# A hybrid attention, DeltaNet and expert trunk on one core: another order of steps at the start, in the scan, in the router and in the norms

## The chip, the cores and the metric

The kernel runs on one core of one Trainium2 chip. The metric is the device time of one execution in microseconds (us); the kernel before was run three times. All arithmetic is in float32.

## The reference, cut to what matters

Two groups of tokens go through the same two layers: 128 context tokens and 512 sample tokens, 640 in all, of width 1024.

```python
for l in range(DEPTH):                                   # 2 layers
    sh1, sc1, ga1, sh2, sc2, ga2 = adaln(cond, w_mod[l], b_mod[l])      # silu(cond) @ w_mod + b_mod
    p = rmsnorm(x, g_norm1[l]) * (1 + sc1) + sh1
    glu, q, k, v, dn_qkv, dn_z, dn_ab = split_projection(p @ w_in[l])
    out_a = conformer_conv(glu, ...)                     # depthwise convolution of 31 taps
    out_b = attention(q, k, v, ...)                      # neighbourhood (sample) or full (context)
    out_c = gated_deltanet(dn_qkv, dn_z, dn_ab, ...)     # chunked scan, forward and backward
    x = x + ga1 * (concat(out_a, out_b, out_c) @ w_out[l])
    h = rmsnorm(x, g_norm2[l]) * (1 + sc2) + sh2
    gates = top2_of_best_group(h @ router_wg[l], h @ router_we[l])      # 16 experts in 4 groups
    x = x + ga2 * sum_e gates[e] * (silu(h @ w1[l,e]) * (h @ w3[l,e])) @ w2[l,e]
y = rmsnorm(x, g_final)
```

The outputs are y for both groups, the context's keys and values, and the final states of the scan.

## The kernel before, in words

The kernel is written as one program per engine (`@block.sync`, `tensor`, `scalar`, `vector`, `gpsimd`); each runs its instructions in the order of the text, and semaphores (`need(signal, n)`, `wait_ge`) tie them together. That written order and the semaphores are what sets the order of the work; there is no planner. Two layers are unrolled in Python.

- **Tiles.** x is kept transposed, `xT` (128 partitions x 8 tiles of features x 640 tokens). `hT` (in `hreg`) holds squares, then the normalized x. Weights go through three ring buffers of 2 MB, filled by SP's queue.
- **Start.** SP loads all constants, x, c and c_ctx, then the four first modulation loads (`ring_load(("mod", n))`, 2 MB each), then the input projection's weights. TensorE (PE) turns x. ACT's queue issues the 17 small loads of parameters (`load_params`, L1203) and the copy of the relative bias (L1232) when c has been turned. PE multiplies the four modulation loads (`mod_rows`, L618; `mod_turn`, L624), then turns the parameters (L638, L639), then sums the squares of x over features with a matmul of ones (`norm_sums`, L645, L646). DVE clears three padded buffers (L1597, L1598) at the layer's start, adds the modulation's bias (L1614, L1616) and multiplies x by the inverse root (`norm_one`, L1620); ACT scales and shifts (L1251, L1252); the projection is L656 and L657.
- **DeltaNet.** Five chunks j of 128 tokens, two directions d. Between chunks, PE turns the block inverse (`turn_inverse`, L852) that POOL computes in 30 small steps (`diag_inverse`, L2202, L2203) and DVE spreads into blocks (`inverse_spread`, L1827). Before it, DVE updates the state of both directions (L1913, L1918 or L1921); behind it follow the level matmuls (L865, L876, L878). POOL also prepares decayed keys and queries (L2181, L2174).
- **Router.** After the output projection (L1022, L1023) the squares are summed, the logits of 20 columns made in two matmuls per token chunk (L1049 and, for a constant row, L1050), and DVE selects groups and experts in many small steps (L1991 to L2021). Normalization 2 is shared: DVE has tiles 0 and 1 (tile 1 after the selection), POOL tiles 2 to 7 (L2232). PE sums ranks (L1055 to L1058) and turns the tokens (L1069); they are stored to `hx`, gathered for the first blocks (L2239) and scattered to `xs` (L2249). `turn_block` (L1081) turns a block of gathered tokens, ACT copies it (L1501).
- **Experts.** A loop over at most 13 pairs of blocks with `If`/`Else` on the number in use; 8 or 9 are in use. ACT stores each block's output to `ys` (L1505). In the `Else` branch every engine only advances its semaphores; ACT waits there for the stores (L1534).
- **Combination.** POOL gathers each token's two outputs (L2259) when all stores and empty slots have been counted; DVE weighs them per chunk of 128 tokens (`weigh`, L2108, L2109), PE turns the sum (L1158), DVE adds it to `xT` (L2121). After the fifth chunk comes the next layer's normalization, or the final one: squares over all 640 tokens (L1543), sums (L1164, L1165), root (L1545, L1547), product (L2126), transposes to token layout (L1172), copies (L1551), and two stores of y (L1554, L1555).

The lines that a sentence can't give are the end of `norm(1)` on ACT and the empty slots:

```python
for k in range(KD) if n == 0 else (0, 2, 3, 4, 1, 5, 6, 7):      # order of the scaled tiles
    if n == 0:
        need(norm_x, k + 1)              # DVE's product
    elif k < 2:
        need(norm_x, KD + k + 1)
    else:
        need(norm_xp, k - 1)             # POOL's product
...
with act.Else():
    for sig, n in ((sil_ready, 0), (xg_copied, 2), (hid_copied, 0)):
        wait(pr, sig, n, 2)
        act.sem_inc(sig.sem, 2)
    for q in range(2):
        wait(pr, ys_stored[q], 0, 16)
        act.sem_inc(ys_stored[q].sem, 16)
```

## Time and profile before

| what | value |
|---|---|
| median of 3 runs | 2068.96 us (2057.93 to 2071.48) |
| profiled execution, its own time | 2063.77 us |
| span in the profile, first to last instruction | 2061.7 us, 22012 instructions |
| granted TensorE clock, mean | 0.905 |
| PE busy | 1758.6 us (85%) |
| DVE, ACT, POOL busy | 845.3, 476.1, 286.3 us |

The profile is of one execution. PE is the TensorE's matmuls, PEld its weight loads, DVE, ACT and POOL the vector, scalar and GpSimd engines, SP the engine that issues most loads; a trailing q stands for an engine's issue of DMAs. Times in rows are us from the start of the span.

### The profile page before, as it was taken

What the parts mean: (1) busy time and instruction counts of PE and PEld (TensorE: products, weight loads), DVE (VectorE), ACT (ScalarE), POOL (GpSimd) and SP (SyncE); (2) the same over time, 40 slices, a digit from 0 to 9 for tenths busy, and PEclk for the clock granted to TensorE, in tenths of its full rate; (3) what the DMA queues carried; (4) which work ended last, traced back from release to release, by engine and by line L of the source; (5) the groups of instructions that cost most, each with busy time, mean ns of one, the idle gap of its engine ahead of it and who ended that gap; (6) DMA issues with size and microseconds to landing.
All of it is one profiled execution on the core that took longest, in us unless ns stands there. A gap on an engine that the chain in (4) does not pass through costs nothing. (4 is left out here: it accounts for less than half of the span.)

```text
span 2061.7 us, 22012 instructions
## 1 busy us (share of the span) xinstructions
PE 1758.6 (85%) x8309; PEld 1129.0 (55%) x8309; DVE 845.3 (41%) x1626; ACT 476.1 (23%) x850; POOL 286.3 (14%) x450
## 2 busy tenths in 40 slices
PE   4899996987988985999589999797889888699965
PEld 2455663645877553554345566464678844454433
DVE  2169304556666322111326930456576533211114
ACT  1211003353221212222031110335322021222112
POOL 0000213013442012000220000001442201200010
PEclk8899997998999996999689999898899998799986
DMA  9321796920000107999552111450000010799952
GB/s 356 61 82 41 238 281 226 345 72 1 1 1 1 53 21 260 373 362 379 185 132 82 41 62 41 136 211 1 1 1 1 1 53 21 293 386 365 370 210 106
DMA packets 113911, 301.80 MB, mean 146 GB/s; under 512 B 27904, under 2 KB 35746, under 8 KB 100642
## 3 DMA queue, kind: packets, MB, share of 16 engines
q1 hardware_dynamic: 65424, 218.16, 28.5%
q0 software_dynamic: 14080, 53.48, 7.8%
q10 hardware_dynamic: 34322, 28.99, 4.9%
q8 instruction: 58, 0.95, 0.2%
q14 instruction: 27, 0.22, 0.0%
HBM read 234.51 MB, written 67.05 MB: 146 GB/s over the span
## 5 line engine op out<-in xcount | busy, mean ns | idle before, releaser
L656 PE MATMUL ps<-hreg,ring 128*128 128x512 f32 x768 | 399.5, 602 | 7.7 <-ACT hreg L1252 7.7
L657 PEld LDWEIGHTS ps<-hreg,ring 128*128 128x128 f32 x768 | 147.7, 192 | 187.1 <-issue 187.1
L1097 PE MATMUL ps<-ring,tok 128*128 128x512 f32 x544 | 238.3, 596 | 0.5 <-issue 0.4
L1097 PEld LDWEIGHTS ps<-ring,tok 128*128 128x128 f32 x544 | 103.9, 192 | 131.5 <-issue 131.5
L657 PE MATMUL ps<-hreg,ring 128*128 128x128 f32 x768 | 149.0, 276 | 0.0
L656 PEld LDWEIGHTS ps<-hreg,ring 128*128 128x128 f32 x768 | 118.6, 195 | 8.0 <-issue 8.0
L1112 PE MATMUL ps<-ring,work 128*128 128x512 f32 x272 | 122.4, 592 | 0.0
L2087 DVE TENSOR_TENSOR work<-work,ps 128x256 f32<-128x256 f32 x34 | 14.3, 421 | 252.8 <-ACT work L1510 252.8
L1649 DVE SCALAR_TENSOR_TENSOR mixA<-cin_reg,small,mixA 128x655 f32<-128x655 f32 x120 | 107.1, 895 | 0.0
L2091 DVE COPY zs<-ps 128x1024 f32<-128x1024 f32 x34 | 41.6, 1225 | 119.9 <-PE ps L1112 119.9
L2164 POOL TENSOR_TENSOR hreg<-dnT,cst 128x512 f32<-128x512 f32 x16 | 20.4, 1274 | 483.8 <-DVE dnT L1851 483.8
L1663 DVE SCALAR_TENSOR_TENSOR tmp_reg<-mixb_reg,small,tmp_reg 128x642 f32<-128x642 f32 x96 | 84.7, 882 | 0.0
L1112 PEld LDWEIGHTS ps<-ring,work 128*128 128x128 f32 x272 | 49.1, 191 | 48.8 <-issue 48.8
L1081 PE MATMUL ps<-cst,tok 128*128 128x128 f32 x304 | 43.8, 291 | 29.7 <-DMA tok<-hx,idx 27.5
L2259 POOL DMA_INDIRECT hreg<-ys,slots x10 | 11.8, 1180 | 406.3 <-ACTq L1535 403.8
L1022 PE MATMUL ps<-dnT,ring 128*128 128x512 f32 x128 | 65.5, 594 | 0.0
L1158 PE MATMUL ps<-cst,hreg 128*128 128x128 f32 x80 | 19.6, 427 | 49.2 <-DVE hreg L2109 49.2
L852 PE MATMUL ps<-cst,ring 128*128 128x128 f32 x80 | 17.6, 368 | 47.6 <-DVE ring L1827 47.6
L1081 PEld LDWEIGHTS ps<-cst,tok 128*128 128x128 f32 x304 | 39.7, 197 | 30.7 <-issue 27.6
L1287 ACT ACTIVATE mixb_reg<-ps 128x512 f32<-128x512 f32 x24 | 14.3, 597 | 174.1 <-PE ps L657 174.1
L1945 DVE SCALAR_TENSOR_TENSOR xT<-ps,small,xT 128x512 f32<-128x512 f32 x16 | 12.0, 751 | 103.4 <-PE ps L1023 103.4
L618 PE MATMUL ps<-ring,small 128*32 128x512 f32 x384 | 48.7, 629 | 6.6 <-DMA ring<-in_w_mod 4.9
(350 smaller groups left out, 3058.0 us busy)
## 6 DMA issues: line engine op xcount, KB each, us to landing
ring<-in_w SPq DMA_DIRECT2D x102, 1024.0 KB, 8.1
ring<-in_w_mod SPq DMA_DIRECT2D x24, 2048.0 KB, 8.3
ring<-in_w_in SPq DMA_DIRECT2D x12, 2048.0 KB, 7.9
ys<-zs ACTq DMA_DIRECT2D x34, 512.0 KB, 7.9
tok<-xs SPq DMA_DIRECT2D x30, 512.0 KB, 9.5
xs<-zero POOLq DMA_DIRECT2D x8, 1792.0 KB, 19.6
ys<-zero POOLq DMA_DIRECT2D x8, 1664.0 KB, 18.5
ring<-in_w_out SPq DMA_DIRECT2D x4, 2048.0 KB, 8.0
```

Of the source, the lines that this page charges most:

```text
L618: ins = mm(bank(bnk)[32 * j:32 * j + 32], condT[:, k, :], w[:, k, :], start=k < 4, stop=k >= 4)
L656: mm(o[:, 0:TS], lhs(k), rhs(k)[:, 0:TS], start=k == 0, stop=k == nk - 1)
L657: ins = mm(o[:, TS:T], lhs(k), rhs(k)[:, TS:T], start=k == 0, stop=k == nk - 1)
L1022: mm(gslot(gg % 2)[:, 0:TS], lhs, mix(k)[0], start=k == 0, stop=k == KD - 1)
L1081: ins = turn(ps[:, P * k:P * (k + 1)], xg[q].rearrange("p (m k) -> p k m", k=KD)[:, k], ident)
L1097: ins = mm(bank(2 + q), xgT[q][:, k, :], w, start=k == 0, stop=k == KD - 1)
L1112: ins = mm(bank(4 + 2 * q + n), hidT[:, P * f:P * (f + 1)], ring[2][:, 2048 * q + D * f + 512 * n:2048 * q + D * f + 512 * n + 512], start ...
L1158: ins = turn(ps[:, o:o + P], yg[0][c_][:, P * k:P * (k + 1)], ident)
L1649: last[t] = count(V.scalar_tensor_tensor(mixA[:, t, :], src, w, mixA[:, t, :], ALU.mult, ALU.add))
L1663: ins = V.scalar_tensor_tensor(out, src, w, out, ALU.mult, ALU.add)
L2091: V.tensor_copy(ysb[q], ps[:, 2048 + 1024 * q:3072 + 1024 * q]).then_inc(y_out.sem, 1)
L2164: G.tensor_tensor(rcos[t % 2], dnT[:, qk_tile(t), 0:TS], cst[:, C_COS:C_COS + TS], ALU.mult).then_inc(rope_cos.sem, 1)
```

## The change

1. **Start.** The constants are loaded in three pieces, the cosine, sine and mask tables behind the third modulation load. c and c_ctx are loaded into `dsm`. ACT issues the parameter loads and the bias copy of layer 0 before its first wait. In layer 0 the square sums are made between the modulation matmuls into the first banks, and the parameters are turned behind the third modulation; DVE's memsets follow the modulation's sums.
2. **Scan.** `inverse_spread(j + 1)` stands between the two directions' state updates.
3. **Router.** The constant row is spread over partitions by two matmuls inside the output projection and added by DVE when it reads the logits. DVE makes tiles 0 to 3 of normalization 2 before the selection, POOL tiles 4 to 7. The second `turn_block` uses other banks.
4. **Empty slots.** ACT counts the stores without waiting for them there.
5. **Norms after the experts.** Squares and sums of layer 1's first normalization are made per chunk. The final one is made in token layout: per chunk a transpose, a square with its row sum, logarithm and exponential of one column, one product with the gain from a loaded row, one store by SP.

```diff
+            for a, b in ((0, C_COS), (C_COL, NC)):
+                sp.dma_start(cst[:, a:b], consts[:, a:b]).then_inc(once["cst_loaded"], 16)
...
-            sp.dma_start(prm[0:8, 0, :], c[0].rearrange("(k p) -> k p", p=P)).then_inc(once["first_loaded"], 16)
+            sp.dma_start(dsm[0:8, 0:P], c[0].rearrange("(k p) -> k p", p=P)).then_inc(once["first_loaded"], 16)
...
                     for n in range(MOD_FIRST):
                         ring_load(("mod", n))
+                        if n == 2:
+                            sp.dma_start(cst[:, C_COS:C_COL], consts[:, C_COS:C_COL]).then_inc(once["cst_loaded"], 16)
...
+                if l == L - 1:
+                    sp.dma_start(g_row, g_final.rearrange("(a n) -> a n", a=1).to_broadcast([P, D])).then_inc(once["g_loaded"], 16)
...
+            for c_ in range(NCH):
+                sp.wait_ge(once["fin_y"], c_ + 1)
+                rows_ = y_sample[0][tokens(c_), :] if c_ < TS // P else y_prompt[0]
+                sp.dma_start(rows_, yg[0][c_]).then_inc(once["y_stored"], 16)
...
                         if n:
                             mod_turn(n - 1, first_rows[n - 1], 3072 + 8 * (n - 1))
+                        if n == 1:
+                            norm_sums(range(0, 4), 0)
+                        if n == 2:
+                            norm_sums(range(4, KD), 0)
+                            params_turn()
                     mod_turn(3, first_rows[3], 3072 + 24)
...
+                    if m == 2:
+                        need(logit_copied, 1)
+                        for g_ in range(2):
+                            ins = mm(ps[:, 2940 + 20 * g_:2960 + 20 * g_], ident[0:2, g_:g_ + 1].to_broadcast([2, P]), crow,
+                                     start=True, stop=True)
...
-                    mm(o, lrow[:, P * t:P * (t + 1)], route_c[:, X_SEL:X_SEL + 20], start=True, stop=False)
-                    ins = mm(o, ident[0:2, g_:g_ + 1].to_broadcast([2, P]), crow, start=False, stop=True)
+                    ins = mm(o, lrow[:, P * t:P * (t + 1)], route_c[:, X_SEL:X_SEL + 20], start=True, stop=True)
...
-                need(xg_copied, 1)
                 need(xf_loaded[1], 16)
-                turn_block(1)
+                turn_block(1, 2048)
...
+                def next_sums(c_):
+                    pe.wait_ge(sq_ready.sem, sq_ready.at(l + 1, c_ + 1 if c_ + 1 < NCH else KD))
+                    for k in range(KD):
+                        ins = mm(ps[:, 2048 + P * c_:2048 + P * (c_ + 1)], ones, yg[0][c_][:, P * k:P * (k + 1)],
+                                 start=k == 0, stop=k == KD - 1)
...
+                def last_turn(c_):
+                    need(comb_added, c_ + 1)
+                    if c_ >= 2:
+                        pe.wait_ge(once["fin_y"], c_ - 1)
+                    for k in range(KD):
+                        o = 2048 + 1024 * (c_ % 2) + P * k
+                        ins = turn(ps[:, o:o + P], xT[:, k, tokens(c_)], ident)
+                    ins.then_inc(once["y_turned"], 1)
+                finish = next_sums if l + 1 < L else last_turn
...
+                    if c_:
+                        finish(c_ - 1)
+                finish(NCH - 1)
...
+            load_params(0)
+            bias_copy(0)
+            act.wait_ge(once["cst_loaded"], 32)
...
-                    for k in range(KD) if n == 0 else (0, 2, 3, 4, 1, 5, 6, 7):
+                    for k in range(KD):
...
+                        for q in range(2):
+                            act.sem_inc(ys_stored[q].sem, 16)
                         for sig, n in ((sil_ready, 0), (xg_copied, 2), (hid_copied, 0)):
...
-                        for q in range(2):
-                            wait(pr, ys_stored[q], 0, 16)
-                            act.sem_inc(ys_stored[q].sem, 16)
+                nc.scalar.preload_act_table_set("natural_log_exp_and_others")
+                if l + 1 < L:
+                    for c_ in range(NCH):
+                        need(comb_added, c_ + 1)
+                        A_(yg[0][c_].rearrange("p (k n) -> p k n", k=KD), xT[:, :, tokens(c_)], ACT.Square)\
+                            .then_inc(sq_ready.sem, 1 if c_ + 1 < NCH else KD + 1 - NCH)
...
+            for c_ in range(NCH):
+                act.wait_ge(once["y_turned"], c_ + 1)
+                A_(yg[0][c_], ps[:, 2048 + 1024 * (c_ % 2):3072 + 1024 * (c_ % 2)], ACT.Square,
+                   accum_out=fin_ss[:, c_:c_ + 1]).then_inc(once["fin_sq"], 1)
+                act.wait_ge(once["fin_sq"], 2 * c_ + 1)
+                A_(fin_rs[:, c_:c_ + 1], fin_ss[:, c_:c_ + 1], ACT.Ln, scale=1.0 / D, bias=eps_c).then_inc(once["fin_sq"], 1)
+                act.wait_ge(once["fin_sq"], 2 * c_ + 2)
+                A_(fin_rs[:, c_:c_ + 1], fin_rs[:, c_:c_ + 1], ACT.Exp, scale=-0.5).then_inc(once["fin_r"], 1)
...
-                for s in stage:
-                    V.memset(s, 0.0)
-                V.memset(cin_reg[:, :], 0.0).then_inc(pads_zeroed.sem, 1)
...
                 V.scalar_tensor_tensor(A[0], mod[:, 8:16, :], 1.0, both[:, R_G1:R_G1 + KD].to_broadcast([P, KD, 2]),
                                        ALU.add, ALU.mult).then_inc(mod_ready.sem, 1)
+                if l == 0:
+                    dve.wait_ge(once["cst_loaded"], 48)
+                for s in stage:
+                    V.memset(s, 0.0)
+                V.memset(cin_reg[:, :], 0.0).then_inc(pads_zeroed.sem, 1)
...
                     for d in range(2):
+                        if d == 1 and j < 4:
+                            inverse_spread(j + 1)
...
-                    if j < 4:
-                        inverse_spread(j + 1)
...
+                    if m == 3:
+                        need(logit_rows, 2)
+                        V.tensor_copy(crb[:, 0:4, :], ps[:, 2940:2960].rearrange("p (a n) -> p a n", a=1).to_broadcast([P, 4, 20]))
+                        step(V.tensor_copy(crb[:, 4, :], ps[:, 2960:2980]))
...
-                norm_one(0)
+                for k in range(4):
+                    norm_one(k)
...
-                norm_one(1)
...
+                def last_norm(c_):
+                    dve.wait_ge(once["g_loaded"], 16)
+                    dve.wait_ge(once["fin_r"], c_ + 1)
+                    V.scalar_tensor_tensor(yg[0][c_], ps[:, 2048 + 1024 * (c_ % 2):3072 + 1024 * (c_ % 2)], fin_rs[:, c_:c_ + 1],
+                                           g_row, ALU.mult, ALU.mult).then_inc(once["fin_y"], 1)
...
+                    if l == L - 1 and c_:
+                        last_norm(c_ - 1)
+                if l == L - 1:
+                    last_norm(NCH - 1)
...
-                for k in range(2, KD):
+                for k in range(4, KD):
                     G.tensor_tensor(hT[:, k, :], xT[:, k, :], rst, ALU.mult).then_inc(norm_xp.sem, 1)
```

## Rows read from the trace of the kernel before

**Rows 1.** PE's waits: line, releaser, us in total, times, longest.

```profile
PE ps L852 <- DVE ring L1827: 47.6, 18, 7.3
```

**Rows 2.** Timeline of the start: start, us, engine, line, operation, count, idle before.

```profile
22.68 1.28 DVE L1597 MEMSET mixb_reg<- 128x646 f32 x2 [0.20 <-DVE xT L1569]
...
23.36 0.40 ACTq L1203 DMA_DIRECT2D tmp_reg<-in_b_mod  x1
...
37.34 3.19 PE L618 MATMUL ps<-ring,small 128*32 128x512 f32 x16 [2.87 <-DMA ring<-in_w_mod]
...
40.46 1.95 PE L624 MATMUL ps<-cst,work 128*128 128x2 f32 x16
...
54.66 0.47 PE L638 MATMUL ps<-cst,tmp_reg 128*128 128x128 f32 x1 [12.26 <-DMA small<-in_router_we]
...
68.79 5.97 DVE L1620 TENSOR_TENSOR hreg<-xT,rst 128x640 f32<-128x640 f32 x8 [12.69 <-ACT rst L1242]
...
71.00 2.04 PE L656 MATMUL ps<-hreg,ring 128*128 128x512 f32 x2 [3.83 <-ACT hreg L1252]
```

**Rows 3.** Stretches: busy by engine, PE clock, DMA share, GB/s.

```profile
5.00:10.00 5.00, 0.00 (x0) 0.00 (x0) 0.00 (x0) 0.00 (x0) 0.00 (x0) 1.00 0.98 399
...
35.00:40.00 5.00, 2.66 (x16) 0.68 (x16) 0.00 (x0) 0.00 (x0) 0.00 (x0) 0.66 1.09 351
```

**Rows 4.** Timeline of the first chunk boundary of the DeltaNet, layer 0.

```profile
529.38 0.68 DVE L1918 COPY dnT<-ps 128x512 f32<-128x512 f32 x1
...
530.10 1.04 POOL L2181 TENSOR_TENSOR tmp_reg<-tok,small 128x512 f32<-128x512 f32 x1
...
532.65 2.93 DVE L1827 TENSOR_TENSOR ring<-dsm,cst 128x512 f32<-128x512 f32 x2
534.06 0.63 PE L852 MATMUL ps<-cst,ring 128*128 128x128 f32 x4 [3.08 <-DVE ring L1827]
...
536.61 1.91 PE L865 MATMUL ps<-work,hreg 128*128 128x128 f32 x8
```

**Rows 5.** Stretches around two chunk boundaries and one behind the scan.

```profile
526.00:546.00 20.00, 15.87 (x116) 15.50 (x115) 12.95 (x32) 6.00 (x14) 8.09 (x17) 0.83 0.00 1
565.00:585.00 20.00, 15.88 (x127) 15.51 (x126) 13.77 (x34) 6.00 (x14) 8.57 (x19) 0.91 0.00 1
686.00:688.00 2.00, 0.29 (x1) 0.29 (x2) 0.94 (x2) 1.62 (x3) 0.00 (x0) 1.00 0.33 115
```

**Rows 6.** Timeline of the routing, layer 0.

```profile
764.86 9.58 POOL L2232 TENSOR_TENSOR hreg<-xT,rst 128x640 f32<-128x640 f32 x6 [116.64 <-ACT rst L1242]
765.56 1.52 DVE L1620 TENSOR_TENSOR hreg<-xT,rst 128x640 f32<-128x640 f32 x1
...
771.53 1.45 DVE L1993 SCALAR_TENSOR_TENSOR small<-small,cst 128x20 f32<-128x20 f32 x1
...
783.68 6.87 PE L1069 MATMUL ps<-cst,hreg 128*128 128x128 f32 x40 [2.49 <-ACT hreg L1252]
...
810.45 1.97 PE L1081 MATMUL ps<-cst,tok 128*128 128x128 f32 x8 [1.11 <-ACT tok L1501]
```

**Rows 7.** DMA issues behind layer 0's last pair: queue, count, KB each, us to landing.

```profile
ys<-zs ACTq DMA_DIRECT2D x2, 512.0 KB, 2.6
```

**Rows 8.** Timeline from layer 0's last store to layer 1's projection.

```profile
998.25 0.34 ACTq L1505 DMA_DIRECT2D ys<-zs  x1
1005.65 0.95 POOL L2259 DMA_INDIRECT hreg<-ys,slots  x1 [191.44 <-ACTq L1535]
...
1029.66 4.31 DVE L2121 SCALAR_TENSOR_TENSOR xT<-ps,small,xT 128x128 f32<-128x128 f32 x16
...
1053.17 1.53 PE L656 MATMUL ps<-hreg,ring 128*128 128x512 f32 x2 [3.84 <-ACT hreg L1252]
```

**Rows 9.** Timeline of the last layer's combination.

```profile
2014.98 1.28 DVE L2109 SCALAR_TENSOR_TENSOR hreg<-dnT,small,hreg 128x1024 f32<-128x1024 f32 x1
...
2024.28 4.30 DVE L2121 SCALAR_TENSOR_TENSOR xT<-ps,small,xT 128x128 f32<-128x128 f32 x16
```

More of the change, by code:

```diff
@@ L599, in _ @@
                 ins.then_inc(once["pe_first"], 1)
-            turn(bank(4, 16), prm[0:16, 0, :], ident[0:16, 0:16]).then_inc(once["cond_turned"], 1)
+            turn(bank(4, 16), dsm[0:16, 0:P], ident[0:16, 0:16]).then_inc(once["cond_turned"], 1)
             pe.wait_ge(once["x_turned"], KD)
@@ L626, in mod_turn, with params_turn, norm_sums @@
                     ins.then_inc(mod_turned, 1)
+                def params_turn():
+                    need(prm_loaded, 16 * PRM_DMAS)
+                    turn(bank(7, P), prm[:, 0, :], ident)
+                    turn(ps[:, 3584 + P:3584 + P + NROW2], prm[0:NROW2, 1, :], ident[0:NROW2, 0:NROW2]).then_inc(prm_turned.sem, 1)
+                def norm_sums(tiles, lo):
+                    for k in tiles:
+                        need(sq_ready, k + 1)
+                        mm(ps[:, lo:lo + TS], ones, hT[:, k, 0:TS], start=k == 0, stop=k == KD - 1)
+                        ins = mm(ps[:, lo + TS:lo + T], ones, hT[:, k, TS:T], start=k == 0, stop=k == KD - 1)
+                        if k == KD - 1:
+                            ins.then_inc(norm_ss.sem, 1)
                 if l == 0:
@@ L1542, in _ @@
-            for k in range(KD):
-                A_(hT[:, k, :], xT[:, k, :], ACT.Square).then_inc(once["fin_sq"], 1)
-            act.wait_ge(once["fin_ss"], 1)
-            A_(rst[:, 0:T], ps[:, 2048:2048 + T], ACT.Ln, scale=1.0 / D, bias=eps_c).then_inc(once["fin_r"], 1)
-            act.wait_ge(once["fin_r"], 1)
-            A_(rst[:, 0:T], rst[:, 0:T], ACT.Exp, scale=-0.5).then_inc(once["fin_r"], 1)
-            yt = xload
-            for k in range(KD):
-                act.wait_ge(once["y_turned"], k + 1)
-                A_(yt[:, :, k * P:(k + 1) * P], gslot(k % 2).rearrange("p (c n) -> p c n", c=NCH), ACT.Copy)\
-                    .then_inc(once["y_copied"], 1)
```

102 lines of the change are left out of this document (39 added, 63 removed).

## The prediction, made before the changed kernel was run

> **What bounds the kernel now.** I read the waits of TensorE (PE) first, then the timeline at the places they name, then windows there for the granted clock. PE is busy most of the time, so what can be won lies where it stands still. Five kinds of place do that, and the change touches each: the start, the chunk boundaries of the DeltaNet scan, the routing, the passage from layer 0 to layer 1, and the end. The reader should see in each group which instruction ends the wait.
>
> *Start* [rows 2]: the last of four modulation loads (mod 3) is used at 37.34, its rows are turned by 42.4, but PE then stands 12.26 us until 54.66 for the parameter list, whose first load was issued only at 23.36. Then come the two parameter transposes, the modulation sums on DVE, the square sums, the root, the product with it (68.79) and the first projection matmul at 71.00. The transfers behind this fill the DMA engines [rows 3].
>
> *DeltaNet* [rows 1, 4]: at a chunk boundary PE waits for inverse_spread (L1827), 47.6 us in 18 waits; two per layer belong to the first chunk and are not touched, leaving four boundaries per layer.
>
> *Routing, passage, end* [rows 6 to 9]: PE waits for normalized tiles, for the stores of the experts' outputs, for a whole normalization after the last combined chunk.
>
> **Start.** The parameter list is issued ahead of everything on ACT's queue, c and c_ctx get a place of their own (dsm), and 1 MB of constants goes behind mod 2. The bytes ahead of mod 3 stay the same, but the whole list now shares the engines with them. Before, part of it did so after mod 3. DMA moved 399 GB/s without the list and 351 GB/s with it [rows 3]: 12% of the 31.3 us from its first issue to its landing is 3.8 us; I charge mod 3 with 1 us (bounds 0 and 4). So mod 3 at 38.3; its rows 3.2 (41.5); copy and turn 1.9, as from 40.53 to 42.41 (43.4); two small DVE operations, taken as 0.4 (estimate; they lie in the 1.5 us from 54.66 to the square sums that the code puts behind them). The squares and square sums need no parameter and move between the modulation matmuls, where PE waited for loads. The three memsets of the padding, before under a DVE that stood idle, now stand behind the modulation sums and ahead of the product: two at 0.64 and one of 1370 columns, by columns 1.36, so 2.6 us in all (46.4). From the product's start to the first matmul is 2.2 (68.79 to 71.00): 48.6. Gain 22.4. What is queued behind the memsets on DVE is exactly that product, so they are paid in full. ACT can start its first function only when it has issued 18 DMAs; from the first issue to the last landing is 31.3, which bounds that issue from above, and I take 21 (estimate), about when x has been turned. Bounds of the start: 13 (issue or DMA cost 10 more) to 24.
>
> A rule of the skill speaks against this part. The Trainium skill, "DMA: Bandwidth & Descriptors", section "Specifications", asks for transfers of 512 B or more for line rate; router and gate rows are 16 to 64 B. By it the list could cost the engines more than the 12%; the trace agrees that there is a loss, and rival C carries what it would do.
>
> **DeltaNet boundaries.** inverse_spread(j+1) moves ahead of the state update of direction 1. DVE is through with direction 0 at 530.06 and POOL's inverse is done at about 530.1 [rows 4], so it can run at once instead of at 532.65. POOL's next operation (530.10, 1.04 us) holds it up: the two spreads took 2.93 beside POOL, each ending about 0.6 behind the end of one POOL operation. So direction 0 ends at 531.8 (before 534.06) and direction 1 at 532.8. Two transposes and a copy later L865 starts at 533.7 against 536.61: 2.9 us each. The state update of direction 1 slips by 2.6 us; its reader comes after some ten matmul groups, so that costs nothing; if POOL were late, it would be the first to be late too. At the fourth, ahead of the context's chunk, two memsets of the state stand there as well and no row is shown; between 0 and 2.9 I take 1.7. Per layer 3x2.9+1.7 = 10.4, both 20.8.
>
> Then the clock. PE idles 3 us there and its granted clock falls: over 20 us it was 0.83 or 0.91; of the first three boundaries of both layers two read like the one row, four like the other [rows 5]. At the lower level (1.2 of 2.4 GHz) that is 6.8 us and 3.6 us, of which half is lost: 2x3.4+4x1.8 = 14. After the change PE idles about 0.8 and 0.5. The nearest row is 686 to 688: busy only 0.29 of 2 us, clock 1.00 throughout [rows 5]. I take it that the clock stays: 14 back (bounds 0 and 20).
>
> The Trainium skill, "TensorE: Matmul & The Clock Gate", section "A second HAM failure mode: psum-queue depth-cycling", tells of short idle spells between matmul groups that come often enough to make the clock swing between its levels. By that rule nothing of the 14 would come back; the row of 686 speaks against it here. It is rival B.
>
> **Routing.** POOL's share of the products falls from six tiles to four (6.4 us instead of 9.58), DVE takes four at once instead of one and, after the selection, another [rows 6]. Beside POOL such a product took 1.52 where the eight at the start took 0.75, and a DVE operation of 20 columns 1.45 while POOL ran: two-input operations end up waiting for POOL's. So DVE is through at 765.56+4x1.52 = 771.6, POOL at 771.3, and the selection's small steps, which before were held until 774.4, run free: about 1.2 us sooner. ACT has all eight tiles by about 778 (five scalings behind 771.6, each at most the 1.4 that the 2.2 at the start leave beside a product), ahead of the ranks. PE's token transposes no longer wait 2.49 for it (783.68). The second block's transposes go to other banks, so the wait of 1.11 at 810.45 goes. 2.5+1.2+1.1 = 4.8, less two small matmuls (0.6, estimate) that the router's constant row adds inside the output projection: 4.2 per layer, 8.4 in both (bounds 4 and 13). The row's removal from the logits saves only what the four products already cover: nothing. DVE's two table copies lie under a projection group: nothing.
>
> **Passage.** In the empty expert slots ACT waited for the last store and then ran through its slots: store issued 998.25 with 0.34, landing 2.6 later (1001.2), gather called 0.8 ahead of 1005.65. The slots' 3.65 us now start at 998.6 and overlap the landing: 2.6 sooner, in both layers [rows 7, 8].
> The last addition ends at 1033.97 (T), the first matmul comes at 1053.17: 19.2. After: one square of 1024 columns 1.1; eight 128-column matmuls, 3.8 at the lower clock by the nearest row (four took 1.91 [rows 4]) or 1.9 at full; the parameter transposes and DVE's pieces 1.5; memsets 2.6; product to matmul 2.2: T+11.2 or T+9.3. Gain 8.0 to 9.9; I take 9. The other four chunks' squares and sums lie under DVE's weighing; the second table load and the bias copy under PE's sums. 11.6 in all.
>
> **End.** Adds end at 2028.58 now [rows 9]. After: 2.6 sooner by the stores; three products with the final gain ahead of the last add, each 1.28 plus 0.03 by the 128x1024 operation: 2029.9. Then eight transposes 2.0 (as at 810.45), square 1.1, two one-column functions 0.5, the last product 1.3, store issue and landing 0.34+2.6, which was the price of the same 512 KB in [rows 7]; some 0.6 to the end: 2038.4 against 2061.7. Gain 23.3 (bounds 20 and 25). The four other stores and the load of the final gain lie under this or under the projection.
>
> **Sum.** 22.4+20.8+14+8.4+11.6+23.3 = 100.5 off the profiled execution's 2063.8: 1963. The runs shown have their median 5 above that execution and their fastest 6 below, so I name 1965, and the range goes by it. DVE, ACT and POOL work that the change moves is hidden elsewhere by PE's matmuls; the dense stages and expert pairs, most of the time, are unchanged.
>
> **Rivals.**
> A, the forecast: 1950 to 1982, 0.60.
> B, the clock still falls at the boundaries: 14 less, 1979; 0.18.
> C, the list's small rows hold the modulation loads up: 10 more, mod 3 at 48, 1975; 0.09. For: engines are full there. Against: the list landed within 31 us beside 8 MB of loads.
> D, the change does not do what it says in the DeltaNet: the spread waits for POOL as long as before, or the delayed update is missed. PE then waits as now: 35 less, 2000; 0.08. For: POOL's end and DVE's are within 0.1 us. Against: POOL's next operations are of 1.04 us, and one of them is all it waits for.
> E, slower: PE, fed earlier, is granted the lower clock in the dense projections. Each such microsecond loses half; it decides from 2x100 us on, slower by over 1% from about 240. At 300 us: 1963+150 = 2113. Against: at every boundary it was back at full within 6.8 us [rows 5]. 0.02.
> The remaining 0.03: several gains at their lower bounds, inside or near 1%.
>
> Range 1943 to 1992: A with its bounds and the runs' spread, B, C. Beyond it lie D, E and the rest, and A's ends. A measurement of this kernel can tell about 1% from no change; faster by over 1%: 0.95, within 1%: 0.03, slower: 0.02.
>
> **What would show it.** First projection matmul near 49 (C: near 58, with the third modulation's matmuls late); L852's wait near 1 us and windows of 20 us behind it with the clock near 1.00 (B: still 0.83 to 0.91; D: waits of 3 us); transposes in the routing directly behind the rank sums; about 10 us between the last addition of layer 0 and the projection; 10 us from the last addition to the end instead of 33. Wrong would be: a new wait of PE for the update of direction 1, DVE's product behind memsets later than 47, or the adds of the last layer slower than 5.5 us a chunk.

## The result, and the profile after

The changed kernel took 1987.8 us (median of 4 runs, 1983.3 to 1990.7) against 2066.3 for the kernel before (4 runs on the same chip, 2057.9 to 2071.5): a ratio of 0.962, 95% interval 0.958 to 0.966. The span fell from 2061.7 to 1984.7 us. The prediction was 1965, range 1943 to 1992, faster at 0.95. The direction is as forecast and the time is in the range, but the gain is 77 us where the sum had 100.5. Where the other 23 went is what the experiments are for.

The first lines of the page after the change, and PE's longest waits (line, releaser, us in total, times, longest):

```profile
span 1984.7 us, 22021 instructions
...
PE 1726.3 (87%) x8313; PEld 1109.2 (56%) x8313; DVE 856.5 (43%) x1631; ACT 473.9 (24%) x850; POOL 287.3 (14%) x446
```

```profile
PE ps L1203 <- DVE hreg L2148: 36.5, 6, 15.4
PE ps L875 <- DVE ring L1863: 32.0, 20, 7.4
PE ps L1108 <- DMA tok<-hx,idx: 27.1, 4, 12.7
PE ps L1082 <- DVE small L2062: 21.0, 2, 10.5
...
PE ps L1130 <- DVE work L2126: 2.2, 1, 2.2
```

L875 is the L852 of [rows 1]: 47.6 us of waiting became 32.0, of which 15.9 are the waits at the first chunk (7.4 and 0.6 in each layer), which nothing touched. L1082 and L1130 are new or longer: PE waits 10.5 us a layer for the selection (8.1 at most before), and once for the first block's product.

**Stages.** The next table is worked out from the timelines: the first start of one line to the first start of another on PE, in us, both layers where there are two numbers. Lines of the changed kernel: first projection matmul L680; projection and attention L680 to L849; scan L849 to L1023; selection L1070 to L1096; first pair L1124 to L1139; passage L1203 to L680; end from L1203 in layer 1 to the end of the span. The kernels e1 to e9 are the experiments below.

| kernel | first matmul | proj. + attention | scan | selection | first pair | passage | end |
|---|---|---|---|---|---|---|---|
| before | 71.0 | 390.8 / 378.5 | 218.7 / 221.1 | 21.8 / 22.3 | 15.9 / 15.8 | 38.8 | 52.3 |
| e7, before + move | 70.4 | 392.5 / 379.1 | 205.8 / 205.8 | 22.3 / 22.3 | 17.7 / 15.7 | 38.3 | 52.3 |
| after | 52.6 | 394.5 / 381.7 | 206.2 / 206.2 | 19.3 / 19.3 | 18.3 / 15.6 | 29.6 | 30.9 |
| e1, move undone | 53.9 | 390.8 / 381.7 | 218.7 / 216.8 | 19.3 / 19.3 | 19.7 / 15.1 | 29.1 | 30.7 |
| e2, POOL holds | 55.5 | 394.0 / 382.7 | 197.5 / 198.9 | 19.2 / 19.3 | 17.9 / 15.5 | 28.8 | 31.1 |
| e3, memsets early | 51.5 | 394.1 / 379.7 | 207.7 / 205.0 | 19.3 / 19.3 | 19.3 / 16.3 | 26.3 | 31.5 |
| e4, small rows late | 50.0 | 394.5 / 381.8 | 208.7 / 203.5 | 19.3 / 19.3 | 18.7 / 14.9 | 29.3 | 30.2 |
| e5, DVE alone | 54.5 | 394.6 / 382.7 | 207.0 / 206.0 | 17.5 / 17.5 | 19.7 / 15.1 | 29.7 | 30.8 |
| e6, list early | 53.1 | 393.9 / 381.5 | 207.9 / 206.2 | 19.3 / 19.3 | 16.6 / 16.0 | 29.3 | 31.7 |
| e8, four together | 46.2 | 394.0 / 381.6 | 201.8 / 199.1 | 17.5 / 17.5 | 18.0 / 15.0 | 27.1 | 30.8 |
| e9, and list cut | 46.8 | 393.9 / 378.1 | 199.4 / 198.9 | 17.5 / 17.5 | 16.0 / 16.1 | 26.4 | 31.2 |

The columns that an edit doesn't touch show how far one execution differs from another: 1 to 2 us in most, about 4 to 5 in projection and attention.

### The profile page after: what moved, and what is told of

The parts are those of the page before. It is cut to its first block and busy times, and to the rows that moved or that the text cites. A ratio compares the mean times of both kernels' runs of the same rounds, so it can differ in the third digit from the quotient of the medians.

```text
span 1984.7 us, 22021 instructions
## 1 busy us (share of the span) xinstructions
PE 1726.3 (87%) x8313; PEld 1109.2 (56%) x8313; DVE 856.5 (43%) x1631; ACT 473.9 (24%) x850; POOL 287.3 (14%) x446
## 5 line engine op out<-in xcount | busy, mean ns | idle before, releaser
L680 PE MATMUL ps<-hreg,ring 128*128 128x512 f32 x768 | 401.7, 605 | 11.1 <-ACT hreg L1291 11.1
L1124 PE MATMUL ps<-ring,tok 128*128 128x512 f32 x544 | 237.9, 595 | 0.2 <-issue 0.2
L1124 PEld LDWEIGHTS ps<-ring,tok 128*128 128x128 f32 x544 | 103.9, 191 | 130.9 <-issue 130.9
L680 PEld LDWEIGHTS ps<-hreg,ring 128*128 128x128 f32 x768 | 119.0, 196 | 11.4 <-issue 11.4
L1139 PE MATMUL ps<-ring,work 128*128 128x512 f32 x272 | 122.4, 592 | 0.0
L1139 PEld LDWEIGHTS ps<-ring,work 128*128 128x128 f32 x272 | 49.1, 191 | 48.8 <-issue 48.8
L1108 PE MATMUL ps<-cst,tok 128*128 128x128 f32 x304 | 43.8, 291 | 27.1 <-DMA tok<-hx,idx 27.1
L1540 ACT ACTIVATE tok<-ps 128x1024 f32<-128x1024 f32 x38 | 38.9, 1025 | 51.7 <-PE ps L1108 48.0
L633 PE MATMUL ps<-ring,small 128*32 128x512 f32 x384 | 47.3, 614 | 3.8 <-issue 2.1
## 6 DMA issues: line engine op xcount, KB each, us to landing
xs<-zero POOLq DMA_DIRECT2D x8, 1792.0 KB, 19.7
```

Of the source, the lines that this page charges most:

```text
L633: ins = mm(bank(bnk)[32 * j:32 * j + 32], condT[:, k, :], w[:, k, :], start=k < 4, stop=k >= 4)
L680: mm(o[:, 0:TS], lhs(k), rhs(k)[:, 0:TS], start=k == 0, stop=k == nk - 1)
L1108: ins = turn(ps[:, a + P * k:a + P * (k + 1)], xg[q].rearrange("p (m k) -> p k m", k=KD)[:, k], ident)
L1124: ins = mm(bank(2 + q), xgT[q][:, k, :], w, start=k == 0, stop=k == KD - 1)
L1139: ins = mm(bank(4 + 2 * q + n), hidT[:, P * f:P * (f + 1)], ring[2][:, 2048 * q + D * f + 512 * n:2048 * q + D * f + 512 * n + 512], start ...
L1540: A_(xgT[q], ps[:, a:a + D].rearrange("p (k n) -> p k n", k=KD), ACT.Copy).then_inc(xg_copied.sem, 1)
```

## The experiments

Each is the changed kernel with the edit shown, except e7. Ratios are to the kernel before on the same chip; for the changed kernel it was 0.9622.

### e1: the move in the scan undone; e7: the move alone

```diff
-                        if d == 1 and j < 4:
-                            inverse_spread(j + 1)
...
+                    if j < 4:
+                        inverse_spread(j + 1)
```

> The changed kernel with one part undone: inverse_spread(j + 1) stands again behind both directions' state updates, as in the kernel before. In the two traces the stretch from the first chunk's level matmuls to the end of the scan is 11.5 us shorter after the change in layer 0 and 14.9 us in layer 1, of which about 2.5 us in layer 1 fall before the first boundary and belong to the clock there. Theory: the move alone makes the rest, 22 to 25 us, most of it as waits of TensorE (2.8 us at each of six boundaries, 0.7 to 1.3 at the two ahead of the context's chunk), the clock's part being about 5. Then this kernel takes about 2011 us (2009 to 2014), with waits of about 3.1 and 1.0 us at each boundary and low-clock stretches of 3.4 to 6.8 us at all of them. Rival, the forecast's own term: 35 us, 2023. Second rival, the scan became shorter because of something else that moved it (the clock's phase, say): under 10 us, below 1998.

e7 is the same edit the other way round, in the kernel before.

> The kernel before with one part of the change alone: inverse_spread(j + 1) between the two directions' state updates. Theory: the move makes the scan 12 to 13 us shorter in each layer (218.7 and 221.1 us from its first matmul to the output's norm in the kernel before, 206.2 in both layers after) and no other stage differs by more than its granted clock: 25 us less than before, 2036 (2033 to 2039). Rival, the forecast's term: 35 less, 2026. Second rival, a part of the scan's gain in the changed kernel hung on the other parts: 15 or less, 2046 and more. Its other stages are a second look at the kernel before: the stretch from the first projection matmul to the scan was 390.8 and 378.5 us there and 390.8 to 394.5 and 379.7 to 382.7 in five profiles with the change. If it is within 1 us of 390.8 and 378.5 again, the change has lengthened that stretch by some 3 us a layer; if it is nearer to 394 and 382, the difference is that of single executions.

e1 took 2008.2 us, ratio 0.9738 [0.9706, 0.9770]; e7 took 2040.2, ratio 0.9885 [0.9861, 0.9909]. Taken away from the one it costs 0.0116 and given to the other it gains 0.0115: 24 us both ways, so the move works by itself and does not hang on the other parts. The 35 of the forecast is out. (e1's time lies just under the 2009 to 2014 expected of it; the 24 us by the ratios lie within the 22 to 25.) PE's waits for the spread, in e1 and then in e7:

```profile
PE ps L875 <- DVE ring L1863: 47.2, 18, 7.3
...
PE ps L852 <- DVE ring L1827: 31.6, 20, 7.3
```

Some 15 to 16 of the 24 us are these waits (47.2 to 32.0, and 47.6 to 31.6); about 8 remain for the clock. Stretches of 20 us from the first two boundaries of layer 0 (PE, PEld, DVE, ACT, POOL busy, PE clock, DMA share, GB/s), after the change and then in e1:

```profile
510.00:530.00 20.00, 17.64 (x140) 16.89 (x139) 16.13 (x39) 6.00 (x14) 8.86 (x18) 0.91 0.00 1
549.00:569.00 20.00, 17.65 (x145) 15.71 (x144) 18.12 (x36) 4.96 (x13) 6.51 (x9) 1.00 0.01 1
...
510.00:530.00 20.00, 15.88 (x116) 15.51 (x114) 12.54 (x30) 5.81 (x14) 7.31 (x14) 0.83 0.00 1
549.00:569.00 20.00, 15.53 (x122) 14.96 (x120) 13.77 (x33) 5.99 (x14) 7.79 (x16) 0.91 0.00 1
```

e1 has the clock of [rows 5] again, 0.83 and 0.91. After the change it was 0.91 at the first and 1.00 at the second boundary (and at the third, in both layers). Over both scans PE is busy 363.4 us in e1 and 355.6 after the change, with the same number of matmuls: these 7.8 us are the clock's part.

### e2: POOL holds until both spreads are made

```diff
                     diag_inverse(j + 1)
+                    need(dn_xt, 2 * (j + 1) + 2)
                     key_decay(j + 1)
```

> The changed kernel with one wait added: POOL begins the decayed keys of the next chunk only when DVE has made both spreads. In the trace of the changed kernel the two spreads take 2.96 us beside POOL's key operations, and TensorE waits 0.90 and 0.82 us for them at a boundary; the shortest such spread in the kernel before, without a POOL operation beside it, took 0.69. Theory: the spreads are slow only because POOL runs beside them. Alone they take 0.7 each, direction 0 is ready 0.8 us sooner and direction 1 1.6 us sooner, TensorE's two waits nearly go: 1.5 us at each of six boundaries and perhaps 0.5 to 1.5 at the two ahead of the context's chunk, 10 to 12 us in all: about 1977 us. Rival: POOL's keys and queries, begun 1.4 us later, become what TensorE waits for within the chunk, and the gain is given back: 1985 to 1992, with a new wait for POOL. Second rival: the spreads take 1.5 us without POOL as well (their shape, not POOL, sets it): no change in their mean, 1988 to 1995.

1973.5 us, ratio 0.9567 [0.9536, 0.9597]: 11 us less than the changed kernel, with intervals that just overlap. First boundary of layer 0, the timeline after the change and then in e2:

```profile
514.48 1.04 POOL L2226 TENSOR_TENSOR tmp_reg<-tok,small 128x512 f32<-128x512 f32 x1
514.56 2.96 DVE L1863 TENSOR_TENSOR ring<-dsm,cst 128x512 f32<-128x512 f32 x2 [0.17 <-POOL dsm L2248]
515.48 1.49 POOL L2226 TENSOR_TENSOR rst<-tok,small 128x512 f32<-128x512 f32 x1
516.22 0.63 PE L875 MATMUL ps<-cst,ring 128*128 128x128 f32 x4 [0.90 <-DVE ring L1863]
517.67 0.63 PE L875 MATMUL ps<-cst,ring 128*128 128x128 f32 x4 [0.82 <-DVE ring L1863]
518.13 1.08 PE L888 MATMUL ps<-work,hreg 128*128 128x128 f32 x6
...
516.80 1.29 DVE L1863 TENSOR_TENSOR ring<-dsm,cst 128x512 f32<-128x512 f32 x2
517.63 1.23 PE L875 MATMUL ps<-cst,ring 128*128 128x128 f32 x8
518.17 1.04 POOL L2226 TENSOR_TENSOR tmp_reg<-tok,small 128x512 f32<-128x512 f32 x1 [1.41 <-DVE ring L1863]
519.04 1.13 PE L888 MATMUL ps<-work,hreg 128*128 128x128 f32 x8 [0.18 <-ACT work L1454]
```

Two spreads take 2.96 us beside POOL and 1.29 alone; PE's two waits are gone (L875 runs its eight transposes in one go). POOL begins 1.4 later and its operations are 1.04 each instead of 1.04 and 1.49, and no wait for POOL appears. The waits for L1863 fall from 32.0 to 19.2 us, by 12.8, and the scan from 206 to 198 in each layer, by 16 in these two profiles. The rest of the 16 goes with the clock, which stayed at full over all boundaries of both layers (1.00 from 510 to 640 and from 1450 to 1580). By the ratios of the runs the gain is 11 us, inside the 10 to 12 expected.

The Trainium skill, "SBUF — State Buffer", section "Who interferes with whom", says that a DVE operation with two SBUF inputs contends with a GpSimd operation that reads SBUF, and that what they share is an exclusive lock. This pair agrees, 2.96 us against 1.29.

### e3: memsets at the layer's start

```diff
                 need(gemm_done, 0)
+                for s in stage:
+                    V.memset(s, 0.0)
+                V.memset(cin_reg[:, :], 0.0).then_inc(pads_zeroed.sem, 1)
```

> The changed kernel with the three memsets of the padding back at the start of the layer, ahead of the modulation copies, where DVE stands idle. Theory: in the changed kernel they stand between the modulation sums and the product and are paid in full: 47.85 to 50.48 in layer 0, and in layer 1 the product starts at 12.26 after the hundred (1012.26) where the root is there at 1010.06. Gone from there, the first projection matmul comes 2.6 us sooner in layer 0 and 2.2 in layer 1: 4.8 in all, about 1983 us. Rival: something else ends just behind (the weights of the projection, the root), and less than 1.5 us in all is won: 1987.

1981.2 us, ratio 0.9602 [0.9572, 0.9633]; the intervals overlap, so the stages decide. The passage is 26.3 instead of 28.8 to 29.7 in the others with the memsets where the change put them: 3. In layer 0 the fourth modulation came at 45.10 there, 1.6 later than after the change, and the first matmul 1.1 sooner: 2.7. The two lines in e3 (those after the change stand under e4):

```profile
45.10 1.93 PE L633 MATMUL ps<-ring,small 128*32 128x512 f32 x16
...
51.53 1.99 PE L680 MATMUL ps<-hreg,ring 128*128 128x512 f32 x2 [2.63 <-ACT hreg L1291]
```

Both as the theory says: the memsets were paid in full.

### e4: small rows and the bias copy behind the first weights

```diff
-            load_params(0)
-            bias_copy(0)
+            load_params(0, act, True, False)
...
                     ring_load(("in", l, c_))
+                    if l == 0 and c_ == 0:
+                        bias_copy(0, sp)
+                        load_params(0, sp, False, True)
```

The first call issues the ten loads that PE turns, the second the other seven, which have a semaphore of their own.

> The changed kernel with only the ten parameter loads that TensorE turns issued at the start; the other seven loads of the list (rows of 16 to 64 bytes, about 3,700 packets) and the copy of the bias go to SP's queue behind the first weights of the input projection. The third modulation is used at 34.53 and the fourth at 43.46 in the changed kernel, against 30.08 and 37.34 before, and the transfers moved 328 to 362 GB/s from 5 to 30 us against 367 to 402 before. Theory: the small rows hold up the modulation loads. Without them the fourth is used 2.5 to 4 us sooner (39.5 to 41), the first projection matmul comes at 49 to 50 instead of 52.6, and the time is about 1984.5. Rival: the loss comes from the ten loads of 512-byte rows and from the constants being cut into pieces of shorter rows; then the rate from 5 to 15 us stays at about 330 and the fourth modulation at 42.5 or later: 1987 or more. Second rival: the first weights or the bias, held up by the small rows, come too late, and the start is no sooner or later than 52.6.

1982.7 us, ratio 0.9610 [0.9579, 0.9642]; again the stages decide. The rate of the transfers, after the change and then in e4:

```profile
10.00:15.00 5.00, 0.09 (x1) 0.12 (x2) 0.00 (x0) 0.00 (x0) 0.00 (x0) 1.00 0.96 328
20.00:25.00 5.00, 2.86 (x20) 2.00 (x18) 3.50 (x5) 1.38 (x2) 0.00 (x0) 1.00 1.11 350
...
10.00:15.00 5.00, 0.49 (x3) 0.52 (x4) 0.00 (x0) 0.00 (x0) 0.00 (x0) 1.00 1.04 392
20.00:25.00 5.00, 3.08 (x26) 2.06 (x28) 3.11 (x4) 2.17 (x3) 0.00 (x0) 1.00 1.05 387
```

So the small rows do slow the transfers. But in most profiles that is not what the start waits for. Timeline after the change (L633 multiplies the modulation loads), then the fourth modulation and the first matmul in e4, then the first modulation in e1:

```profile
17.49 6.01 ACTq L1215 DMA_DIRECT2D bias_pad<-in_na_rel_bias  x1
23.61 1.28 ACT L1248 ACT_TABLE_LOAD   x1 [23.61 <-PE ps L615]
25.19 3.64 PE L633 MATMUL ps<-ring,small 128*32 128x512 f32 x32 [2.09 <-issue]
34.53 1.92 PE L633 MATMUL ps<-ring,small 128*32 128x512 f32 x16 [0.28 <-DMA ring<-in_w_mod]
43.46 1.92 PE L633 MATMUL ps<-ring,small 128*32 128x512 f32 x16 [1.42 <-DMA ring<-in_w_mod]
50.48 5.90 DVE L1656 TENSOR_TENSOR hreg<-xT,rst 128x640 f32<-128x640 f32 x8
52.62 2.05 PE L680 MATMUL ps<-hreg,ring 128*128 128x512 f32 x2 [5.36 <-ACT hreg L1291]
...
40.81 1.92 PE L668 MATMUL ps<-ring,small 128*32 128x512 f32 x16
49.97 2.05 PE L715 MATMUL ps<-hreg,ring 128*128 128x512 f32 x2 [5.36 <-ACT hreg L1298]
...
27.02 4.98 PE L633 MATMUL ps<-ring,small 128*32 128x512 f32 x32 [4.07 <-issue]
```

PE waits 1.70 us for modulation loads after the change, and not at all in e1, e2, e3, e5, e6 and e4. In the first five of those it waits 3.6 to 5.2 us ("issue") in front of the first modulation, because ACT's SiLU stands behind ACT's own DMA issues, which end there at 24.4 to 25.6; the first modulation then runs in part at the lower clock (4.98 us in e1, 3.64 after the change). Behind that PE is busy without a gap: eight pairs of square sums of 1.08 each, 8.7 us, lie between the modulations. e4 takes the issues away and the small rows at once, so that no run parts the two. By the timelines it was the issue in those five: their fourth modulation comes at 43.96 to 46.37, 3 to 6 us later than in e4, without a wait for a load. After the change itself it was the loads, 1.70 of the 2.65 us; there ACT's issues ended at 23.50, only 0.4 us behind PE's last transpose ahead of the SiLU (L615).

### e5: all eight products of normalization 2 on DVE

```diff
-                for k in range(4):
+                for k in range(KD):
                     norm_one(k)
...
-                for k in range(4, KD):
-                    G.tensor_tensor(hT[:, k, :], xT[:, k, :], rst, ALU.mult).then_inc(norm_xp.sem, 1)
```

> The changed kernel with all eight products of normalization 2 on DVE ahead of the selection, none on POOL. In the changed kernel four products on DVE and four on POOL run side by side and both engines take 1.94 us for each (7.76 and 7.77 us), and DVE reads the logits only at 748.54; at the start of the layer DVE alone took 5.90 us for eight, 0.74 each. Theory: the two engines hinder each other, and DVE alone is through with eight sooner than both with four: at 740.86 + 5.9 = 746.8. The small steps, the ranks and the token transposes come 1.8 us sooner in both layers, ACT's eight scalings (1.09 each) end at about 751, ahead of the ranks: 3.6 us, less what layer 0 gives back where ACT issues the next layer's loads: 1984 to 1986. Rival: DVE takes 1.5 or more for each product beside ACT's scalings too, and the selection starts at 753 or later: 1996 or more. Second rival: the scalings end after the ranks and hold up the token transposes: no gain, 1988.

1983.7 us, ratio 0.9601 [0.9576, 0.9626]. Timeline of layer 0, after the change and then in e5:

```profile
740.16 7.77 POOL L2277 TENSOR_TENSOR hreg<-xT,rst 128x640 f32<-128x640 f32 x4 [118.18 <-ACT rst L1281]
740.86 7.76 DVE L1656 TENSOR_TENSOR hreg<-xT,rst 128x640 f32<-128x640 f32 x4
748.54 0.25 DVE L2039 TENSOR_TENSOR small<-ps,work 128x100 f32<-128x100 f32 x1
753.82 0.71 PE L1082 MATMUL ps<-small,cst 128*128 128x80 f32 x2 [10.51 <-DVE small L2062]
...
743.01 5.96 DVE L1653 TENSOR_TENSOR hreg<-xT,rst 128x640 f32<-128x640 f32 x8
748.89 0.26 DVE L2036 TENSOR_TENSOR small<-ps,work 128x100 f32<-128x100 f32 x1
754.18 0.71 PE L1081 MATMUL ps<-small,cst 128*128 128x80 f32 x2 [9.74 <-DVE small L2059]
```

One engine makes eight products in 5.96 us; two engines make four each in 7.77. The selection takes 17.5 us instead of 19.3 in both layers, the 1.8 expected. In the time it is 4 us, with overlapping intervals.

### e6: the next layer's list ahead of the token copies

```diff
+                if l + 1 < L:
+                    load_params(l + 1)
                 copy_tokens(0, 0)
                 copy_tokens(0, 1, 2048)
-                if l + 1 < L:
-                    load_params(l + 1)
```

> The changed kernel with the loads of layer 1's parameters issued before ACT's two copies of gathered tokens instead of behind them. In layer 0 of the changed kernel ACT issues these 17 loads from 782.77 to 796.64 (11.4 us in the kernel before, 13.9 here), its first SiLU comes only at 799.14, and TensorE waits 2.18 us for the product behind it; the stretch from the first up projection to the first down projection is 18.3 us in layer 0 and 15.6 in layer 1, where no list is issued. Theory: the list stands ahead of the SiLU on ACT's queue and took back 2.5 us of what the routing had gained. In the 15.6 us that ACT waits for the gathered tokens it costs nothing: that stretch falls to 15 to 16 us in layer 0, the time to about 1985. Rival: the list's small rows then share the engines with the scattered and gathered tokens, TensorE waits longer than 12.5 us for the first block, and nothing is won: 1988 or more. Second rival: the first up projection, not ACT, sets that stretch: no change.

1991.0 us, ratio 0.9650 [0.9625, 0.9676]: nothing won, rather some 6 us lost by the ratio (the intervals overlap). ACT's queue and what waits for it, after the change and then in e6:

```profile
793.61 1.89 ACTq L1241 DMA_DIRECT2D small<-in_w_in  x1
795.52 1.12 ACTq L1241 DMA_DIRECT2D small<-in_router_we  x1
797.85 1.28 ACT L1549 ACT_TABLE_LOAD   x1 [14.06 <-issue]
800.04 0.50 PE L1130 MATMUL ps<-cst,work 128*128 128x128 f32 x2 [2.18 <-DVE work L2126]
...
773.66 9.41 ACTq L1241 DMA_DIRECT2D small<-in_w_in  x1
783.10 9.52 ACTq L1241 DMA_DIRECT2D small<-in_router_we  x1
793.74 15.61 PE L1124 MATMUL ps<-ring,tok 128*128 128x512 f32 x32 [7.79 <-ACT tok L1540]
```

The theory was right that the list sets the first pair (18.3 fell to 16.6) and wrong on the idle 15.6 us: beside the scatter of tokens, two loads took 9.4 and 9.5 us to issue instead of 1.9 and 1.1, and PE stood 7.8 us for ACT's copies.

### e8 and e9: what the experiments point to

e8 has the edits of e2 to e5 together. In e9 ACT issues, besides, only ten of layer 1's loads, and SP the other seven behind layer 1's first weights.

> The changed kernel with four of the edits together: POOL waits for both spreads, the memsets stand at the layer's start, the small rows and the bias copy go to SP's queue behind the first projection weights, and DVE makes all eight products of normalization 2. Alone they gave, as differences of the ratio to the kernel before, 0.0055, 0.0020, 0.0012 and 0.0021, together 0.0108 of 2062, 22 us. Theory: the places don't touch each other (scan, start and passage, start, routing), so the gains add: a ratio of about 0.951 (0.949 to 0.954), 1964 us. In the profile: first projection matmul at 47 to 48, scan 198 us in both layers, 17.5 us from the square sums to the token transposes. Rival: with the start's loads sooner and the memsets gone, the first projection weights or ACT's scalings set the start (first matmul still at 50), and layer 0's routing gain goes to the wait behind ACT's list of loads (18 to 20 us from the first up projection to the first down projection, as in all runs with the list there): 1968 to 1972.

The edit of e9, against e8:

```diff
-                    load_params(l + 1, act, True, True)
+                    load_params(l + 1, act, True, False)
...
-                        load_params(0, sp, False, True)
+                        load_params(l, sp, False, True)
```

> The four edits together, and in layer 0 ACT issues only the ten turned parameter loads of layer 1 behind the copies of gathered tokens; the seven others follow on SP's queue behind the first projection weights of layer 1. From the first up projection to the first down projection layer 0 took 17.7 to 19.7 us in all profiles with 17 loads in ACT's queue there and 14.9 to 16.3 in layer 1 without. The seven loads are 5 to 6 of ACT's 13.9 us of issue. Theory: ACT's issue sets that stretch, so with ten loads it ends before the first up projection is through (half of it is there 12.3 us after its start) and the stretch falls to 15 to 16 us: 3 us less than the four edits alone, about 1961. Rival: ten loads are still too long or something else delays the SiLU: the stretch stays at 18 or more and the time equals that of the four edits. Second rival: the seven loads, now in front of layer 1's later projection weights, delay these or the gathered outputs, and it is slower than the four edits.

e8: 1960.2 us, ratio 0.9489 [0.9466, 0.9513]. e9: 1955.9, ratio 0.9465 [0.9441, 0.9490]. The gains add, 27 us by the ratio where the four alone had given 22: first matmul at 46 to 47, scan near 199 to 202, selection 17.5. In e9 the first pair of layer 0 takes 16.0 instead of 18.0, as expected, though the two intervals overlap. Both are faster than the changed kernel and than the one before it.

## Why the prediction was right, and where it was off

The time lies in the stated range, but above case A's 1950 to 1982, to which the prediction gave 0.60. The upper end of the range took in rivals B and C, and neither came out in the main. That the time is still inside, at 1988, owes something to luck. What held is the direction and most of the mechanisms; four terms came out smaller than forecast. One of the signs that the prediction named for being wrong did appear: DVE's product behind the memsets came at 50.48, later than 47.

The terms of the sum against the two profiled executions, by the stages above (routing is the stretch from the output projection's first matmul to the first down projection, 139.8 and 140.4 us before and 139.5 and 137.3 after; stores the one from there to the combination, 185.6 and 207.8, then 183.5 and 205.8):

| term | forecast | measured | in single runs of other kernels |
|---|---|---|---|
| start | 22.4 | 18.4 | 15 to 18 with the same start |
| scan | 34.8 | 27.4 | 24 by e1 and e7 |
| projection, attention | 0 | -6.9 | single executions, about -2 a layer |
| routing | 8.4 | 3.3 | |
| stores | 5.2 | 4.1 | |
| passage | 9.0 | 9.2 | 9 to 10 |
| end | 20.7 | 21.4 | 21 to 22 |
| sum | 100.5 | 76.9 | |

**Passage and end: right in their steps.** The last add of layer 0 ends at 1005.20 and the first matmul comes at 1014.40: T+9.2, where the prediction gave T+9.3 for full clock:

```profile
1000.83 4.37 DVE L2166 SCALAR_TENSOR_TENSOR xT<-ps,small,xT 128x128 f32<-128x128 f32 x16
...
1014.40 2.05 PE L680 MATMUL ps<-hreg,ring 128*128 128x512 f32 x2 [5.77 <-ACT hreg L1291]
```

The end went as written, down to the three products ahead of the last add. The last steps of the chain of waits:

```profile
1974.89 2.08 DVE xT L2166 x8
...
1977.02 1.11 PE ps L1193 x8
...
1978.15 1.12 ACT hreg L1584 x2
...
1979.93 1.28 DVE hreg L2154
```

Square 1.1 and product 1.3 stand in the prediction; only the transposes took 1.1 instead of 2.0. From the last add to the end it is 7.7 us, where the kernel before had a whole normalization behind its last add [rows 9], 33.1 us. No run undid these two parts; they rest on the traces alone.

**Stores: right in its step, smaller.** From the last store's issue to the first gather it is 7.40 and 6.61 us in the two layers before, and 5.44 and 4.76 after: 2.0 and 1.9 sooner where the prediction had 2.6. The other profiles with the change have the same within 0.01, and e7 has 7.41 and 6.60.

**Start: two steps failed.** "The squares and square sums ... move between the modulation matmuls, where PE waited for loads." Before, PE waited 2.03 and 2.87 us there [rows 2 show the second]; the sums are 8.7. So they were hidden by half: from the first modulation to the fourth it is 18.3 us instead of 13.9, and the fourth came at 43.46, not 38.3. The other step is ACT's issue, taken as 21: it was 23.5 to 25.6, the SiLU stood behind it, and the SiLU is what PE's first modulation needs. In the profile after the change most of this second loss is something else: the first modulation comes 1.8 us later than before (25.19 against 23.43), and 1.3 of that is there when PE has turned x and starts on c (L615 at 22.87, its like before at 21.55): x lands later, at 328 GB/s from 10 to 15 us where it was 402 before. From the fourth modulation on, the working held: 9.2 us to the first matmul where it had 10.3, and the memsets 2.6. Rival C had its mechanism (the rate did fall), but PE's own work covered most of it, and the 10 us did not come. The rule of the Trainium skill, "DMA: Bandwidth & Descriptors", section "Specifications", on transfers under 512 B is in agreement with e4's rates, 392 against 328 GB/s; in this profile it cost PE the 1.70 us of waits and part of the 1.3, and the sums cost more.

**Scan: right in its mechanism, two sizes off.** At the first boundary PE waits 0.90 and 0.82 us, where the prediction had 0.8 and 0.5, and L888, counted from the last matmuls ahead of the boundary, comes 2.8 us sooner (2.9 in the prediction). That price was then multiplied by three; at the second and third boundary it was about 2.4, at the fourth below 1 instead of 1.7. The waits gave 15.6 where the sum had 20.8. The clock gave about 8 where it had 14. It did not come back everywhere: of the prediction's 28 us at the lower level (two windows of 6.8 and four of 3.6) two windows of 3.6 stayed, so some 21 went. And the step "of which half is lost" was too much: these 21 us gave about 8. PE also stands still in such a stretch (busy 15.9 of 20 us in [rows 5]), at either clock, which would make the loss smaller; that this is the whole reason no run shows. Rival B is out in the main: the windows read 1.00 at four of six boundaries and 0.91 at two, and in e2 1.00 over 130 us of the scan in both layers. So the rule of the Trainium skill that spoke for B ("TensorE: Matmul & The Clock Gate", section "A second HAM failure mode: psum-queue depth-cycling") did not decide here. Rival D is out: DVE waits 0.17 us for POOL.

**Routing: the price beside POOL.** "765.56 + 4 x 1.52" should have been 4 x 1.94: the one product of [rows 6] was taken for the price of four, while the two engines alternate. DVE read the logits 2.9 us later than before, measured from the residual add, and the steps from there to the ranks, 5.2 us instead of 8.0 since POOL no longer ran beside them, only made that good: the ranks came no sooner. What remained is the 2.5 us for which the token transposes had waited; in layer 1, where such a wait also went, the selection is 3.0 shorter. The second block's own banks, with what else lies between the token transposes and the first up projection, gave about 1.5 a layer (28.0 on the mean without the change, 26.5 with it, e6's layer 0 aside), where the prediction had 1.1. In layer 0 the first pair gave 2.4 back: ACT's list of 17 loads in front of the SiLU took 13.9 us to issue instead of 11.4. That the list was there is in the prediction nowhere. But e7, without the routing's change, has 17.7 us there too, so how much of the 2.4 belongs to the change stays open. Another 3.2 were lost in the output projection ahead of the selection; there the means are 74.2 us without the change and 74.4 with it, so this is mostly the difference of two executions.

**Projection and attention: not in the sum.** The nine profiles with the change have 393.8 and 381.3 us in this stretch, the two without it 391.7 and 378.8 (means). By these means 4.6 of the 6.9 go with the change and 2.3 are the difference of two executions. About 1 us a layer is seen: the first projection matmuls run longer at the lower clock, after waits of PE of 5.4 and 5.8 us where it had 3.8. The other 1 to 1.5 a layer stay open. Within attention one stretch of the same instructions (L745 to L751) took between 86 and 95 us, in the main longer in either layer where its granted clock was lower; and e1, which has the change but for the scan, took 390.8 us in layer 0, as the kernel before did, with the same clock in that stretch, 0.93 in both.

## What to carry to other kernels

Work is hidden in a wait only up to that wait's length: put the two numbers beside each other before writing "where PE waits". When two engines take shares of the same element-wise work, measure the share beside the other one running: here one engine alone was faster than both, and PE's waits at six boundaries, 1.7 us each, vanished when one engine let the other go first. An engine that issued many small loads computed nothing meanwhile (14.06 us in front of ACT's SiLU), and how long that took differed with what else the queues carried, so keep such a list away from any instruction that somebody waits for.

## What the runs showed of the hardware that was not expected

- DVE and POOL products of 640 columns: 1.94 us each on both engines side by side, 0.74 on DVE alone (5.96 for eight). What POOL takes for them quite alone no run shows.
- The issue of one load of 1,024 rows of 64 bytes took ACT 0.8 to 2.1 us in the middle of the kernel, 2.5 to 6.7 beside the modulation and projection loads, and 9.4 to 9.5 beside the scatter of tokens.
- The same waits of 0.9 and 0.8 us at a boundary were followed by a fall of the clock in one execution (0.91 over 20 us) and by none in another (e3, 1.00 over the like stretch), with the same instructions in the scan.
